# Inverting the 16x16 diagonal blocks of the delta matrices on VectorE, by way of DRAM, instead of four doubling levels on TensorE

## The chip, the cores and the metric

One core of one Trainium2 chip runs the whole program in one launch. The metric is device time in microseconds (us). TensorE multiplies matrices into PSUM, VectorE and ScalarE do elementwise work and empty PSUM, GpSimd does a little elementwise work and issues some DMAs, SyncE issues the weight loads. Engines run on their own and meet at semaphores.

## The reference, cut to what matters

A decoder block over T = 528 positions (16 meta tokens and 512 inputs), width 2048. Most of the work is projection: `proj = xn @ w_in` (2048 x 14368), two output projections and `w_o`. One branch is a gated delta rule with 16 heads of width 128, in NCH = 9 chunks of C = 64 positions. For each head and chunk a unit lower triangular 64x64 matrix is inverted:

```python
k_beta = k * beta[..., None]
lmat = jnp.where(strict, jnp.einsum('bhncd,bhnsd->bhncs', k_beta, k) * decay, 0.0)
tmat = lax.linalg.triangular_solve(eye + lmat, jnp.broadcast_to(eye, lmat.shape), left_side=True, lower=True)
u_c = jnp.einsum('bhncs,bhnsd->bhncd', tmat, v_beta)
w_c = jnp.einsum('bhncs,bhnsd->bhncd', tmat, k_beta * jnp.exp(gcum)[..., None])
```

Then a scan over the 9 chunks carries a 128x128 state per head.

## The kernel before, in words

**The main stream.** The projection runs in windows: for a column block `cp` of 256 weights, four windows (`c`, `h`), each of eight k tiles. A k tile takes three products (`wh*xh`, `wh*xl`, `wl*xh`, a weight and an input each split into a high and a low part), on two halves of 264 or 258 positions, or on one of 512. ScalarE makes `wh` (`split_hi`) and VectorE `wl` (`split_lo`) in four quarter pieces per window, for the window two ahead, in four buffers. SyncE loads 1 MB of raw weights for every second window, when VectorE has split the load before it in that buffer.

**Hooks.** After every second k tile `window` calls `hook(q)`, so a window has four hooks. The heads go in pairs: the four column blocks of a pair (k, q, v, z) have 64 hooks, and hook number m of pair p calls `delta(p - 1, m)` on TensorE, VectorE and ScalarE, which does one piece of the delta rule of the pair before. The last pair's pieces go into the first gate windows. Each engine's instructions stand in this written order; within a window the split comes first and then the hook, and the convolution (`convolve`, hooks 0 to 3 and 8 to 11 of a column block) last. So a wait in a hook holds back all that its engine has behind it. GpSimd's part runs in a loop of its own over the pairs.

**The inversion.** The two heads of a pair lie on partitions 0 to 63 and 64 to 127. `mq` holds decay times K K^T (and Q K^T) for the 9 chunks, `st` the inverse transposed with its column factor, `tm` the inverse. Hook F0 + 4 = 10 makes level 0 (pairs of rows) on VectorE from factors that GpSimd and a small product of hook 8 (`qd_shift`) prepare. From hook L0 = 13 on come levels of doubling, three hooks each: stage 2 of a level transposes `st` on TensorE and ScalarE copies it to `tm`; stage 0 of the next is `mq * tm`, masked by VectorE into `xm`; stage 1 is `xm * st`, subtracted by VectorE from `st`. Levels 1 to 3 take nine chunks, level 4 and 5 eight, level 5 in 32x32 quarters. At R0 = 28 the scan over the chunks begins, up to O0 = 55, and hook 61 is the last. The v and q transposes (`TOK_ROUNDS`) stand at hooks 13, 16, 19, 22, 25 and 28.

Of the kernel before, what the change touches and what calls it, by code (L numbers as in the profile page):

```python
# [52 lines left out]
LEVELS = 6  # L53
SHORT = 4
# [21 lines left out]
CPAIR = 258  # L76
CEPS = 322
# [3 lines left out]
NCOLS = CLEV + C * LEVELS  # L81
# [9 lines left out]
def constants():  # L91
# [10 lines left out]
    c[:, CPAIR:CPAIR + C] = (s[:, None] % 2 == 0) & (col[None] == s[:, None] + 1)  # L102
    for h in range(2):
        c[:, CHALF + h] = half == h
    for lv in range(LEVELS):
        a, b = s[:, None] >> lv, col[None] >> lv
        c[:, CLEV + C * lv:CLEV + C * (lv + 1)] = (b % 2 == 0) & (a == b + 1)
# [16 lines left out]
def build(nc, x, meta_tokens, norm_w, w_in, conv_w, A_log, dt_bias, pool_mix, pool_scale, dn_norm_w,  # L124
# [3 lines left out]
    g_d = nc.dram_tensor("gate_sum_scratch", (PAIRS, 2, NCH, C), F32, kind="Internal").ap()  # L128

    outer = ExitStack()  # L130
    with outer:
# [68 lines left out]
        pw, px = (vtok[:, :, i * C:(i + 1) * C] for i in range(2))  # L200
# [11 lines left out]
        lvm = lay.tensor("lvm", [LEVELS, C])  # L212
# [118 lines left out]
        pe_gate = sem("pe_gate")  # L331
# [161 lines left out]
        def _(pe):  # L493
# [104 lines left out]
            def delta(d, m):  # L598
# [23 lines left out]
                if m in TOK_ROUNDS:  # L622
# [3 lines left out]
                    if TOK_ROUNDS[m][0] == ("v", 0):  # L626
                        wait(silu_done, 4, 3)
                        wait(qd_pair, 1, 1)
# [4 lines left out]
                if m == F0 + 2:  # L633

                    wait(qd_ready, 1, 1)
                    wait(tok_done, ALL_TOK, K_TOK)
                    pe.wait_ge(masks_loaded, 16)
                    alone()
                    for ph in HALVES:
                        mm = product(pt[ph, 0:NCH], lvm[ph, 0, :], qd[ph, 1, :], True, True)  # L640
                    mm.then_inc(qd_shift, 1)
                lv, stage = level_step(m)
                if lv is not None:
                    for g in range(NG):
                        chunks = group(g, lv)
                        if stage == 0:

                            wait(t_ready, NG * (LEVELS - 1), NG * (lv - 1) + g + 1)
                            alone()
                        if stage == 1:  # L650
                            wait(x_ready, NG * (LEVELS - 1), NG * (lv - 1) + g + 1)
                            alone()
                        if stage == 2:
                            wait(s_ready, NG * LEVELS, NG * lv + g + 1)
                            if lv == 0 and g == 0:
                                wait(mq_ready, NG, NG)
                            alone()
                        for n in range(chunks.start, chunks.stop):
                            i = n - GC * g
                            if stage == 2:  # L660
                                mm = pe.transpose(pg[g][0:C, P * i:P * (i + 1)], st[:, n, :], ident)  # L661
                                continue
                            if lv == LEVELS - 1:
# [13 lines left out]
                        mm.then_inc((x_mm, y_mm, t_tr)[stage], 1)  # L677
# [143 lines left out]
        def _(act):  # L821
# [90 lines left out]
            def delta(d, m):  # L912
# [34 lines left out]
                lv, stage = level_step(m)  # L947
                if stage == 2:

                    for g in range(NG):  # L950
                        chunks = group(g, lv)
# [197 lines left out]
        def _(dve):  # L1149
# [170 lines left out]
            def delta(d, m):  # L1320
# [20 lines left out]
                if m == F0 + 1:  # L1341
# [7 lines left out]
                    wait(qd_ready, 1, 1)  # L1349
                    tt(st[:, :, :], cst[:, CI2:CI2 + C].unsqueeze(1).broadcast_to([P, NCH, C]), bc(qd[:, 1, :], C), ALU.mult).then_inc(s_init, 1)  # L1350

                if m == F0 + 2:
                    wait(qd_shift, 1, 1)
                    tt(qd[:, 2, :], pt[:, 0:NCH], qd[:, 1, :], ALU.mult).then_inc(qd_pair, 1)
                if m == F0 + 4:

# [351 lines left out]
```

## Time and profile before

| | us |
|---|---|
| median of 3 runs (lowest, highest) | 2143.07 (2142.34 to 2145.54) |
| span of the profiled execution | 2142.4 |
| TensorE matmul busy | 2096.9 (98%) |
| VectorE busy | 943.1 (44%) |
| ScalarE busy | 847.2 (40%) |
| GpSimd busy | 116.6 (5%) |
| GpSimd's DMA queue, share of 16 DMA engines | 2.7% |
| SyncE's DMA queue, share of 16 DMA engines | 25.8% |

The profiled execution is 0.7 us from the median. A pair of heads takes 135.5 us (from the first burst after hook 5 of one pair to that of the next, 892.64 to 1028.10). Times with two numbers are start and length in us; a matmul in fp32 leaves two records, so "x36" are 18 products.

### The profile page before, as it was taken

What the parts mean: (1) busy time and instruction counts of PE and PEld (TensorE: products, weight loads), DVE (VectorE), ACT (ScalarE), POOL (GpSimd) and SP (SyncE); (2) the same over time, 40 slices, a digit from 0 to 9 for tenths busy, and PEclk for the clock granted to TensorE, in tenths of its full rate; (3) what the DMA queues carried; (4) which work ended last, traced back from release to release, by engine and by line L of the source; (5) the groups of instructions that cost most, each with busy time, mean ns of one, the idle gap of its engine ahead of it and who ended that gap; (6) DMA issues with size and microseconds to landing.
All of it is one profiled execution on the core that took longest, in us unless ns stands there. A gap on an engine that the chain in (4) does not pass through costs nothing.

```text
span 2142.4 us, 40278 instructions
## 1 busy us (share of the span) xinstructions
PE 2096.9 (98%) x15140; PEld 1805.1 (84%) x15140; DVE 943.1 (44%) x2391; ACT 847.2 (40%) x2476; POOL 116.6 (5%) x139
## 2 busy tenths in 40 slices
PE   6999999999999999999999999999999999999996
PEld 6888899989889798897988987778888888888885
DVE  6333444545555455554555544332222544334333
ACT  5322224445354453543535436432222522223333
POOL 4000000000010000100001000000000000000000
PEclk9999999999999999999999999999999999999998
DMA  6133322122121221212212122243346343435221
GB/s 219 54 125 102 98 80 80 61 76 80 41 95 60 76 76 44 95 59 72 66 60 95 41 84 84 76 131 120 103 140 227 113 128 117 147 126 217 79 78 78
DMA packets 177340, 209.06 MB, mean 98 GB/s; under 512 B 6793, under 2 KB 163298, under 8 KB 176546
## 3 DMA queue, kind: packets, MB, share of 16 engines
q1 hardware_dynamic: 167090, 180.27, 25.8%
q0 software_dynamic: 5504, 18.33, 2.7%
q10 hardware_dynamic: 4608, 8.39, 1.0%
q8 instruction: 115, 1.88, 0.4%
q14 instruction: 23, 0.19, 0.0%
HBM read 188.05 MB, written 18.91 MB: 97 GB/s over the span
## 4 chain that ended last, share of the span: by engine, by line
PE 96%; ACT 1%; issue 1%; DVE 1%; POOL 0%; SPq 0%; DMA 0%; DVEq 0%; ACTq 0%
PE pj L495 81%; PE pg L495 9%; PE pt L495 2%; PE pg L661 2%; PE pt L631 1%; ACT tm L823 0%; PE pg L782 0%; DVE fst L1180 0%; POOL xl L1619 0%; ACT pt L946 0%; DMA prow<-in_dn_norm_w 0%; PE pt L725 0%; PE pg L725 0%; DVE res L1599 0%; DVE xl L1186 0%
## 5 line engine op out<-in xcount | busy, mean ns | idle before, releaser
L495 PE MATMUL pj<-xh,wh 128*128 128x264 f32 (+2 forms) x2688 | 756.6, 336 | 4.1 <-DVE wl L1155 3.0
L495 PE MATMUL pj<-xh,wl 128*128 128x264 f32 (+2 forms) x2688 | 716.9, 321 | 6.0 <-issue 6.0
L495 PE MATMUL pj<-xl,wh 128*128 128x264 f32 (+2 forms) x2688 | 718.9, 322 | 0.0
L1155 DVE TENSOR_TENSOR wl<-raw,wh 128x256 fp32r<-128x256 f32 x896 | 365.5, 439 | 678.4 <-ACT wh L823 678.3
L495 PEld LDWEIGHTS pj<-xh,wh 128*128 128x128 f32 x2688 | 445.4, 189 | 71.0 <-issue 26.4
L495 PEld LDWEIGHTS pj<-xh,wl 128*128 128x128 f32 x2688 | 447.5, 189 | 44.9 <-issue 6.6
L495 PEld LDWEIGHTS pj<-xl,wh 128*128 128x128 f32 x2688 | 447.2, 189 | 34.7 <-issue 1.0
L823 ACT ACTIVATE wh<-raw 128x256 fp32r<-128x256 f32 x896 | 310.6, 406 | 20.4 <-ACT stg L1000 19.3
L823 ACT ACTIVATE wh<-rawb 128x256 fp32r<-128x256 f32 x288 | 97.8, 406 | 182.2 <-PE pj L495 181.2
L495 PE MATMUL pj<-yh,wh 128*128 128x512 f32 x384 | 149.6, 389 | 0.0
L495 PE MATMUL pj<-yh,wl 128*128 128x512 f32 x384 | 149.5, 389 | 0.0
L495 PE MATMUL pj<-yl,wh 128*128 128x512 f32 x384 | 149.5, 389 | 0.0
L1318 DVE SCALAR_TENSOR_TENSOR stg<-xin,convcur,stg 128x528 f32<-128x528 f32 x144 | 112.4, 780 | 0.2
L1470 DVE TENSOR_TENSOR wl<-rawb,wh 128x256 fp32r<-128x256 f32 x192 | 69.6, 420 | 92.2 <-ACT wh L823 92.2
L495 PE MATMUL pj<-mh,wh 128*128 128x512 f32 x256 | 101.3, 396 | 0.0
L961 ACT ACTIVATE oo<-pt,cur 128x128 f32<-128x128 f32 x64 | 23.5, 368 | 195.5 <-PE pt L495 195.5
L495 PE MATMUL pj<-mh,wl 128*128 128x512 f32 x256 | 99.9, 390 | 0.0
L495 PE MATMUL pj<-ml,wh 128*128 128x512 f32 x256 | 99.9, 390 | 0.0
L1000 ACT ACTIVATE stg<-pj 128x512 f32<-128x512 f32 x32 | 19.1, 597 | 174.4 <-PE pj L495 174.4
L495 PEld LDWEIGHTS pj<-yh,wl 128*128 128x128 f32 x384 | 72.1, 188 | 15.1
L495 PEld LDWEIGHTS pj<-yh,wh 128*128 128x128 f32 x384 | 72.1, 188 | 15.0
L495 PEld LDWEIGHTS pj<-yl,wh 128*128 128x128 f32 x384 | 72.1, 188 | 14.8
(202 smaller groups left out, 1904.0 us busy)
## 6 DMA issues: line engine op xcount, KB each, us to landing
raw<-in_w_in SPq DMA_DIRECT2D x112, 1024.0 KB, 5.2
rawb<-in_w_dn_out SPq DMA_DIRECT2D x16, 1024.0 KB, 5.8
rawb<-in_w_o SPq DMA_DIRECT2D x12, 1024.0 KB, 5.5
gates_scratch<-stg ACTq DMA_DIRECT2D x32, 256.0 KB, 2.0
rawb<-in_w_pool_out SPq DMA_DIRECT2D x8, 1024.0 KB, 5.6
gst<-gates_scratch POOLq DMA_DIRECT2D x32, 256.0 KB, 3.0
yraw<-branch_scratch SPq DMA_DIRECT2D x1, 5632.0 KB, 21.4
xt<-in_x SPq DMA_DIRECT2D x4, 1024.0 KB, 7.0
```

What stands on the lines that cost most here:

```text
L495: return pe.matmul(dst, lhs, rhs, start=start, stop=stop)
L631: mm = pe.transpose(pt[:, i * P:(i + 1) * P], src.rearrange("p h c -> p (h c)"), ident)
L661: mm = pe.transpose(pg[g][0:C, P * i:P * (i + 1)], st[:, n, :], ident)
L823: return act.activation(dst, src, ACT.Copy)
L961: act.activation(oo[:, n - 1, :], pt[:, 0:HD], ACT.Copy, scale=cur[:, EG, n:n + 1]).then_inc(o_inter, 1)
L1000: act.activation(gates_sb[c], pj[c][:, 0, :], ACT.Sigmoid).then_inc(proj_evac, 1)
L1155: tt(wl[:, j, 2 * q:2 * q + 2, :], raw[:, 2 * par + h, 2 * q:2 * q + 2, c * P:(c + 1) * P], wh[:, j, 2 * q:2 * q + 2, :].bitcast(F32), ALU ...
L1318: dve.scalar_tensor_tensor(acc, xin[:, src_tap:src_tap + T], w, acc, ALU.mult, ALU.add).then_inc(conv_step, 1)
L1470: tt(bwl[:, u, 2 * q:2 * q + 2, :], rawb[:, u, 2 * q:2 * q + 2, c * P:(c + 1) * P], bwh[:, u, 2 * q:2 * q + 2, :].bitcast(F32), ALU.subtra ...
```

## The change

The inverse of each 64x64 matrix now starts from the inverses of its four 16x16 diagonal blocks; levels 4 and 5 remain. A pair has 2 heads x 9 chunks x 4 blocks = 72 blocks. VectorE scales K K^T by the factor `qd` (one instruction, hook 10), GpSimd stores it to a scratch tensor in DRAM in rows of 256 bytes and loads the blocks back, one block of 256 numbers in each of 72 partitions, in runs of 64 bytes. From hook W0 = 13 on VectorE inverts them by columns: 14 steps of two dependent instructions, three steps per hook, and then a turned copy. GpSimd stores the inverse and its transpose (runs of 64 bytes) into two scratch tensors, whose other places were zeroed once at the start, and loads them as `tm` and `st` (rows of 256 bytes). TensorE waits for all four loads at hook L0 = 24. Level 4 gets small products that update `tm`, in place of the transposes. R0, O0, the token rounds and the main stream stay. The column factor moves into ScalarE's copy to `vn`. The blocks lie in `oo`, which the scan writes only later.

```diff
--- before.py
+++ after.py
...
-LEVELS = 6
-SHORT = 4
+LEVELS = (4, 5)
+NL = len(LEVELS)
+BS = 16
+NB = C // BS
+NBLK = NCH * 2 * NB
+BROW = BS * C + BS
...
+    gram_d = nc.dram_tensor("gram_scratch", (NBLK, BROW), F32, kind="Internal").ap()
+    inv_d = [nc.dram_tensor(f"inverse_scratch{i}", (NBLK, BROW), F32, kind="Internal").ap() for i in range(2)]
...
-        pw, px = (vtok[:, :, i * C:(i + 1) * C] for i in range(2))
+        flat = oo[0:NBLK, :, :].rearrange("p n e -> p (n e)")
+        gblk, wblk, wtr = (flat[:, i * BS * BS:(i + 1) * BS * BS].rearrange("p (a i) -> p a i", a=BS) for i in range(3))
+        tblk = flat[:, 3 * BS * BS:4 * BS * BS]
...
-        L0 = F0 + 7
+        V0 = F0 + 7
+        W0 = F0 + 7
+        NSTEP = 3
+        L0 = W0 + 11
...
-            TOK_ROUNDS[L0 + 3 * i] = [("v", n) for n in range(3 * i, 3 * i + 3)]
-            TOK_ROUNDS[L0 + 9 + 3 * i] = [("q", n) for n in range(3 * i + 1, min(3 * i + 4, NCH))]
+            TOK_ROUNDS[V0 + 3 * i] = [("v", n) for n in range(3 * i, 3 * i + 3)]
+            TOK_ROUNDS[V0 + 9 + 3 * i] = [("q", n) for n in range(3 * i + 1, min(3 * i + 4, NCH))]
...
-            return ((m - L0 + 2) // 3, (m - L0 + 2) % 3) if L0 <= m < R0 else (None, None)
-
-        R0 = L0 + 3 * LEVELS - 3
+            return ((m - L0) // 2, (m - L0) % 2) if L0 <= m < R0 else (None, None)
+
+        R0 = L0 + 2 * NL
...
-                if m == F0 + 2:
-
-                    wait(qd_ready, 1, 1)
-                    wait(tok_done, ALL_TOK, K_TOK)
-                    pe.wait_ge(masks_loaded, 16)
-                    alone()
-                    for ph in HALVES:
-                        mm = product(pt[ph, 0:NCH], lvm[ph, 0, :], qd[ph, 1, :], True, True)
-                    mm.then_inc(qd_shift, 1)
...
+                    if (lv, stage) == (0, 0):
+                        wait(inv_loaded, 64, 64)
+                        pe.wait_ge(masks_loaded, 16)
+                        alone()
...
-                        if stage == 2:
-                            wait(s_ready, NG * LEVELS, NG * lv + g + 1)
-                            if lv == 0 and g == 0:
-                                wait(mq_ready, NG, NG)
...
-                            if stage == 2:
-                                mm = pe.transpose(pg[g][0:C, P * i:P * (i + 1)], st[:, n, :], ident)
-                                continue
...
-                        mm.then_inc((x_mm, y_mm, t_tr)[stage], 1)
+                        mm.then_inc((x_mm, y_mm)[stage], 1)
+                        if (lv, stage) == (0, 1):
+                            for n in range(chunks.start, chunks.stop):
+                                i = n - GC * g
+                                for low, high in QUARTERS:
+                                    mm = product(pg[g][low, 384 + 32 * i:416 + 32 * i], st[low, n, 0:32], xm[low, n, 0:32], True, True)
+                            mm.then_inc(t_mm, 1)
...
-                    for g in range(NG):
-                        chunks = group(g, lv)
-                        wait(t_tr, NG * (LEVELS - 1), NG * lv + g + 1)
-                        for hd in range(2):
-                            src = pg[g][0:C, 0:GC * P].rearrange("p (n h c) -> p n h c", h=2, c=C)[:, chunks.start - GC * g:, hd, :]
-                            ins = copy(tm[HALVES[hd], chunks, :], src)
-                        ins.then_inc(t_ready, 1)
...
-                        copy(vn[:, :], pg[0][:, 128:128 + HD]).then_inc(vn_ready, 1)
+                        act.activation(vn[:, :], pg[0][:, 128:128 + HD], ACT.Copy, scale=qd[:, 1, n:n + 1]).then_inc(vn_ready, 1)
...
-                    tt(st[:, :, :], cst[:, CI2:CI2 + C].unsqueeze(1).broadcast_to([P, NCH, C]), bc(qd[:, 1, :], C), ALU.mult).then_inc(s_init, 1)
...
-                        tt(px[:, group(g), :], kk, pw[:, group(g), :], ALU.mult).then_inc(pair_x, 1)
-                    for g in range(NG):
-                        wait(pair_x, NG, g + 1)
-                        tt(st[:, group(g), :], st[:, group(g), :], px[:, group(g), :], ALU.subtract).then_inc(s_ready, 1)
...
+                if m == F0 + 4:
+                    wait(qd_ready, 1, 1)
+                    wait(mq_ready, NG, NG)
+                    tt(mq[:, :, 0, :], mq[:, :, 0, :], bc(qd[:, 1, :], C), ALU.mult).then_inc(mk_ready, 1)
+                if m == W0:
+
+                    wait(blk_loaded, 16, 16)
+                    dve.tensor_scalar(wblk, gblk, -1.0, None, ALU.mult).then_inc(w_init, 1)
+                    wait(w_init, 2, 1)
+                    dve.memset(wblk.rearrange("p a i -> p (a i)")[:, 0:BS * BS:BS + 1], 1.0).then_inc(w_init, 1)
+                    wait(w_init, 2, 2)
+                if W0 <= m and 1 + NSTEP * (m - W0) < BS - 1:
+                    for j in range(1 + NSTEP * (m - W0), min(1 + NSTEP * (m - W0 + 1), BS - 1)):
+                        rest = BS - 1 - j
+                        own = tblk[:, 0:j * rest].rearrange("p (a i) -> p a i", a=j)
+                        if j > 1:
+                            wait(w_step, BS - 2, j - 1)
+                        tt(own, wblk[:, 0:j, j:j + 1].broadcast_to([NBLK, j, rest]),
+                           gblk[:, j:j + 1, j + 1:BS].broadcast_to([NBLK, j, rest]), ALU.mult).then_inc(w_prod, 1)
+                        wait(w_prod, BS - 2, j)
+                        tt(wblk[:, 0:j, j + 1:BS], wblk[:, 0:j, j + 1:BS], own, ALU.subtract).then_inc(w_step, 1)
+                    if j == BS - 2:
+                        wait(w_step, BS - 2, BS - 2)
+                        dve.tensor_copy(wtr, wblk.rearrange("p a i -> p i a")).then_inc(w_turned, 1)
...
+                        elif lv == 0:
+
+                            wait(t_mm, NG, g + 1)
+                            tt(st[:, chunks, :], st[:, chunks, :], src, ALU.subtract).then_inc(s_ready, 1)
+                            for low, high in QUARTERS:
+                                part = tm[low, chunks, 0:32]
+                                move = pg[g][low, 384:480].rearrange("p (n c) -> p n c", c=32)[:, chunks.start - GC * g:, :]
+                                ins = tt(part, part, move, ALU.subtract)
+                            ins.then_inc(t_ready, 1)
...
-                pool.wait_ge(decay_exp, d + 1)
-                pool.tensor_tensor(pw, dec[:, :, :], cst[:, CPAIR:CPAIR + C].unsqueeze(1).broadcast_to([P, NCH, C]), ALU.mult).then_inc(pair_dec, 1)
-                pool.wait_ge(pair_dec, d + 1)
-                pool.wait_ge(qd_pair, d + 1)
-                pool.tensor_tensor(pw, pw, bc(qd[:, 2, :], C), ALU.mult).then_inc(pair_fac, 1)
+                def rows_of(scratch, h):
+
+                    return scratch.rearrange("(n h b) r -> n h (b r)", h=2, b=NB)[:, h, 0:C * C].rearrange("n (s c) -> s n c", c=C)
+
+                pool.wait_ge(mk_ready, d + 1)
+                pool.sem_inc(pool_gate, 1)
+                for h in range(2):
+                    pool.dma_start(rows_of(gram_d, h), mq[HALVES[h], :, 0, :]).then_inc(mk_stored, 16)
+                pool.wait_ge(mk_stored, 32 * d + 32)
+                pool.sem_inc(pool_gate, 1)
+                pool.dma_start(gblk, gram_d[:, 0:BS * C].rearrange("a (j c) -> a j c", c=C)[:, :, 0:BS]).then_inc(blk_loaded, 16)
+
+                pool.wait_ge(w_turned, d + 1)
+                pool.sem_inc(pool_gate, 1)
+                for scratch, block_of in zip(inv_d, (wblk, wtr)):
+                    pool.dma_start(scratch[:, 0:BS * C].rearrange("a (j c) -> a j c", c=C)[:, :, 0:BS], block_of).then_inc(w_stored, 16)
+                pool.wait_ge(w_stored, 32 * d + 32)
+                pool.sem_inc(pool_gate, 1)
+                for h in range(2):
+                    pool.dma_start(tm[HALVES[h], :, :], rows_of(inv_d[1], h)).then_inc(inv_loaded, 16)
+                    pool.dma_start(st[HALVES[h], :, :], rows_of(inv_d[0], h)).then_inc(inv_loaded, 16)
```

On TensorE, hooks 13 and 14 of a pair before (`pt<-cst,vch` are the v transposes, `pg<-cst,st` the transposes of `st`, `pg<-tm,mq` stage 0 of level 1):

```order
L121 REGISTER_ALU
L631 MATMUL pt<-cst,vch 128x128 x3
L121 ISA x2
L661 MATMUL pg<-cst,st 64x128 x3
L121 REGISTER_ALU
L661 MATMUL pg<-cst,st 64x128 x3
L121 REGISTER_ALU
L661 MATMUL pg<-cst,st 64x128 x3
L495 MATMUL pj<-xh,wh 128x264 x2
```

The same engine in the changed kernel, the end of hook 23 and hook 24, where the wait for the four loads stands ahead of the first product of level 4:

```order
L508 MATMUL pj<-xh,wh 128x258 x2
L508 MATMUL pj<-xl,wh 128x258 x2
L508 MATMUL pj<-xh,wl 128x258 x2
L125 ISA
L508 MATMUL pg<-tm,mq 64x64 x16
L508 MATMUL pj<-xh,wh 128x258 x2
```

Hooks 13 to 23 now hold the v and q transposes alone, and the levels' products begin at hook 24.

On GpSimd, from the decay difference (`dec`) to the first scaled copy of `st` (`sq`), before:

```order
L1656 TENSOR_TENSOR dec<-tm,cur 128x576
L1659 TENSOR_TENSOR vtok<-dec,cst 128x9x64
L1662 TENSOR_TENSOR vtok<-vtok,qd 128x9x64
L1664 ISA
L1665 TENSOR_TENSOR sq<-st,cst 128x384
```

and in the changed kernel:

```order
L1670 TENSOR_TENSOR dec<-tm,cur 128x576
L1679 DMA gram_scratch<-mq 64x9x64 x2
L1682 DMA oo<-gram_scratch 72x16x16
L1687 DMA inverse_scratch<-oo 72x16x16 x2
L1691 DMA tm<-inverse_scratch 64x9x64
L1692 DMA st<-inverse_scratch 64x9x64
L1691 DMA tm<-inverse_scratch 64x9x64
L1692 DMA st<-inverse_scratch 64x9x64
L1694 ISA
L1695 TENSOR_TENSOR sq<-st,cst 128x384
```

Nine DMAs in four groups, each group behind a wait, stand where two elementwise instructions stood.

On VectorE in the changed kernel, the first hook of the inversion (m = 13) and the split of the next hook (`oo` holds the blocks):

```order
L125 ISA
L1357 TENSOR_SCALAR oo<-oo 72x256
L1359 MEMSET oo 72x16
L1367 TENSOR_TENSOR oo<-oo 72x14
L125 ISA
L1370 TENSOR_TENSOR oo<-oo 72x14
L1367 TENSOR_TENSOR oo<-oo 72x26
L125 REGISTER_ALU
L1370 TENSOR_TENSOR oo<-oo 72x2x13
L1367 TENSOR_TENSOR oo<-oo 72x36
L125 REGISTER_ALU
L1370 TENSOR_TENSOR oo<-oo 72x3x12
L1149 REGISTER_ALU
L1150 TENSOR_TENSOR wl<-raw,wh 128x256
```

The wait for the blocks (the first row) stands ahead of these and so ahead of every later split `wl`.

## Rows read from the trace of the kernel before

**Rows 1.** The page: busy time by engine, and the chain that ended last.

```profile
PE 2096.9 (98%) x15140; PEld 1805.1 (84%) x15140; DVE 943.1 (44%) x2391; ACT 847.2 (40%) x2476; POOL 116.6 (5%) x139
PE 96%; ACT 1%; issue 1%; DVE 1%; POOL 0%; SPq 0%; DMA 0%; DVEq 0%; ACTq 0%
```

**Rows 2.** Waits, longest in total: us, times, longest us.

```profile
DVE wl L1155 <- ACT wh L823: 678.3, 261, 9.8
```

**Rows 3.** Chain of waits, hooks 13 to 27 of one pair: start, us.

```profile
904.75 0.33 PE pt L631 x3
905.08 0.98 PE pg L661 x9
906.06 1.45 PE pj L495 x12
907.51 1.20 PE pg L495 x36
908.70 1.67 PE pj L495 x12
910.37 1.20 PE pg L495 x36
...
935.60 1.08 PE pg L495 x32
...
943.73 0.62 PE pg L495 x32
```

**Rows 4.** Timeline of VectorE, hooks 7 to 10 of the same pair.

```profile
895.89 0.17 DVE L1346 TENSOR_TENSOR qd<-cur,rk 128x9 f32<-128x9 f32 x1
896.10 0.17 DVE L1348 TENSOR_TENSOR qd<-qd,rk 128x9 f32<-128x9 f32 x1
896.30 0.76 DVE L1350 TENSOR_TENSOR st<-cst,qd 128x576 f32<-128x576 f32 x1
897.57 0.50 DVE L1315 TENSOR_SCALAR stg<-xin,convcur 128x528 f32<-128x528 f32 x1
901.35 0.41 DVE L1155 TENSOR_TENSOR wl<-raw,wh 128x256 fp32r<-128x256 f32 x1
```

**Rows 5.** Groups by line: GpSimd's DMA issues, busy us and mean ns of one.

```profile
L1682 POOL DMA_DIRECT2D gst<-gates_scratch x32 | 17.2, 538 | 482.5 <-DMA gates_scratch<-stg 270.6 <-DVE merged L1495 211.2
L1647 POOL DMA_DIRECT2D tm<-gate_sum_scratch x16 | 8.4, 528 | 31.3 <-issue 30.8
L1606 POOL DMA_DIRECT2D mixcur<-in_pool_mix x4 | 3.1, 776 | 0.4 <-issue 0.4
L1630 POOL DMA_DIRECT2D gate_sum_scratch<-grow x2 | 1.3, 632 | 0.0
```

**Rows 6.** DMA issues: KB each, median us from issue to landing.

```profile
raw<-in_w_in SPq DMA_DIRECT2D x112, 1024.0 KB, 5.2
gst<-gates_scratch POOLq DMA_DIRECT2D x32, 256.0 KB, 3.0
tm<-gate_sum_scratch POOLq DMA_DIRECT2D x16, 144.0 KB, 2.9
gate_sum_scratch<-grow POOLq DMA_DIRECT2D x2, 18.0 KB, 4.0
```

**Rows 7.** The tile mixcur (256 KB by GpSimd, four loads): landing.

```profile
DMA to landing us min/median/max: 3.2/6.6/7.4
```

**Rows 8.** DMA queue of the weight loads: packets, MB, share of 16 engines.

```profile
q1 hardware_dynamic: 167090, 180.27, 25.8%
```

**Rows 9.** Stretches at the start: length, busy by engine, granted clock (PEclk), DMA.

```profile
27.00:30.00 3.00, 1.07 (x6) 1.11 (x7) 3.00 (x5) 1.19 (x2) 1.11 (x2) 0.83 1.09 386
33.00:36.00 3.00, 0.45 (x3) 0.45 (x4) 2.97 (x6) 2.67 (x6) 2.78 (x3) 0.97 0.01 3
36.00:39.00 3.00, 3.00 (x15) 3.00 (x15) 3.00 (x4) 3.00 (x11) 3.00 (x3) 0.50 0.02 5
39.00:42.00 3.00, 3.00 (x26) 3.00 (x25) 1.97 (x7) 0.46 (x2) 3.00 (x3) 0.96 0.00 0
```

More of the change, by code:

```diff
@@ L75 @@
 CHALF = 256
-CPAIR = 258
-CEPS = 322
+CEPS = 258
 NCONST = CEPS + 1
@@ L80 @@
 CLEV = CHB + P
-NCOLS = CLEV + C * LEVELS
+CZERO = CLEV + C * NL
+NZERO = NBLK * BROW // P
+NCOLS = CZERO + NZERO
 NTILE_CONV = 3 * HEADS
@@ L101, in constants @@
     c[:, CUP:CUP + C] = np.where(s[:, None] <= col[None], 0.0, NEG)
-    c[:, CPAIR:CPAIR + C] = (s[:, None] % 2 == 0) & (col[None] == s[:, None] + 1)
     for h in range(2):
         c[:, CHALF + h] = half == h
-    for lv in range(LEVELS):
+    for i, lv in enumerate(LEVELS):
         a, b = s[:, None] >> lv, col[None] >> lv
-        c[:, CLEV + C * lv:CLEV + C * (lv + 1)] = (b % 2 == 0) & (a == b + 1)
+        c[:, CLEV + C * i:CLEV + C * (i + 1)] = (b % 2 == 0) & (a == b + 1)
     same = half[:, None] == half[None]
@@ L1348, in delta @@
                     tt(qd[:, 1, :], qd[:, 0, :], rk[:, 1, :], ALU.mult).then_inc(qd_ready, 1)
-                    wait(qd_ready, 1, 1)
-                    tt(st[:, :, :], cst[:, CI2:CI2 + C].unsqueeze(1).broadcast_to([P, NCH, C]), bc(qd[:, 1, :], C), ALU.mult).then_inc(s_init, 1)
[L1352 to L1355, printed above, removed]
-                    wait(pair_fac, 1, 1)
-                    wait(s_init, 1, 1)
-                    for g in range(NG):
-                        kk = pg[g][:, 0:GC * 2 * C].rearrange("p (n a c) -> p n a c", a=2, c=C)[:, :, 0, :]
-                        tt(px[:, group(g), :], kk, pw[:, group(g), :], ALU.mult).then_inc(pair_x, 1)
-                    for g in range(NG):
-                        wait(pair_x, NG, g + 1)
-                        tt(st[:, group(g), :], st[:, group(g), :], px[:, group(g), :], ALU.subtract).then_inc(s_ready, 1)
                 if m == F0 + 3:
@@ L1377, in delta @@
                         if stage == 0:
-                            wait(x_mm, NG * (LEVELS - 1), NG * (lv - 1) + g + 1)
+                            wait(x_mm, NG * NL, NG * lv + g + 1)
+                            if (lv, g) == (0, 0):
+                                dve.wait_ge(masks_loaded, 16)
                             pattern = lvm[:, lv, :].unsqueeze(1).broadcast_to([P, chunks.stop - chunks.start, C])
                             tt(xm[:, chunks, :], src, pattern, ALU.mult).then_inc(x_ready, 1)
-                        else:
-                            wait(y_mm, NG * (LEVELS - 1), NG * (lv - 1) + g + 1)
-                            wait(s_ready, NG * LEVELS, NG * (lv - 1) + g + 1)
-                            if lv == LEVELS - 1:
-                                for low, high in QUARTERS:
-                                    part = st[low, chunks, 32:C]
-                                    ins = tt(part, part, src[low, :, 32:C], ALU.subtract)
-                                ins.then_inc(s_ready, 1)
-                            else:
-                                tt(st[:, chunks, :], st[:, chunks, :], src, ALU.subtract).then_inc(s_ready, 1)
+                        elif lv == 0:
[6 more added lines that the diff above has]
+                            ins.then_inc(t_ready, 1)
+                        else:
+                            wait(y_mm, NG * NL, NG * lv + g + 1)
+                            wait(s_ready, NG * NL, g + 1)
+                            for low, high in QUARTERS:
+                                part = st[low, chunks, 32:C]
+                                ins = tt(part, part, src[low, :, 32:C], ALU.subtract)
+                            ins.then_inc(s_ready, 1)
                 if R0 <= m < O0:
@@ L1639, in _ @@
             pool.memset(vch[:, 0, :, 0:PAD], 0.0).then_inc(zeroed, 1)
-            pool.dma_start(lvm[:, :, :], consts[:, CLEV:NCOLS].rearrange("p (l c) -> p l c", l=LEVELS)).then_inc(masks_loaded, 16)
+            pool.dma_start(lvm[:, :, :], consts[:, CLEV:CZERO].rearrange("p (l c) -> p l c", l=NL)).then_inc(masks_loaded, 16)
+            for i in range(2):
+                pool.dma_start(inv_d[i].rearrange("a r -> (a r)").rearrange("(p c) -> p c", p=P), consts[:, CZERO:NCOLS]).then_inc(blk_zeroed, 16)
             def row_load(d):
@@ L1649, in _ @@
             pool.wait_ge(gsum_stored, 32)
+            pool.wait_ge(blk_zeroed, 32)
             pool.sem_inc(work_free, 1)
```

36 lines of the change are left out of this document (17 added, 19 removed).

## The prediction

> **What bounds the kernel now.** I read the page first: TensorE is busy 98% of the span, and the chain that ended last runs 96% through it [rows 1]. The waits say that nobody else presses: VectorE's longest sum of waits, 678 us, is for ScalarE's high parts, and ScalarE makes those only as TensorE frees buffers [rows 2]. So every product that leaves TensorE's queue shortens the span, and every us that TensorE waits lengthens it. Then I read one pair of heads in the chain of waits [rows 3]: bursts of small products stand between the stretches `pj` of the projection, and ScalarE's and VectorE's part of a level fits under the next stretch. TensorE has no reserve of other work at a wait: its queue is in order.
>
> **What the change takes from TensorE, per pair.** From rows 3:
> - transposes of `st` at hooks 13, 16, 19, 22: 4 x 0.98; at hook 25 eight of them, 8/9 of that, 0.87. Together 4.8 us.
> - stages 0 and 1 of levels 1 to 3: six bursts "x36" of 1.20 = 7.2 us. The stretch behind such a burst lasts 1.67, that behind the transposes 1.45, so each burst costs another 0.2: 1.2 us.
> - the small product of hook 8, about 0.2, and a short wait for ScalarE's copies at level 5, about 0.2.
>
> Sum 13.6 us. Added: sixteen 32x32 products at hook 25; a burst of level 5 is as many of that size, 0.62. Net 13.0 us per pair, 8 pairs: 104 us. This is the most that the change can bring: 2143 - 104 = 2039.
>
> **What it puts in its place.** TensorE must have all four loads before hook 24. Follow one pair on the clock of rows 3 and 4.
>
> TensorE's deadline. Hook 24's burst began at 935.6. Ahead of it go 3.9 of transposes, 8.4 of bursts, 0.2 of hook 8 and the burst of hook 23 (1.16 and 0.2, now in hook 24): 13.8. So TensorE would stand at hook 24 at 921.8. Each us that the loads land later is a wait s, and a pair changes by s - 13.0.
>
> The start. VectorE began the split of hook 10 at 901.35 [rows 4]. The instruction of 576 elements at hook 7 (0.76) and a small one go; behind the split (0.41) comes the scaling of K K^T, again 576 elements, 0.76. It ends at 901.35 - 0.9 + 0.41 + 0.76 = 901.6.
>
> From there a chain without a fork: stores A, load B, the inversion C, stores D, loads E. No DMA of before has 576 or 1152 runs, so A, B, D and E are bounded. Issue time on GpSimd: 528 ns for 64 runs, 538 for 128, 632 for 72, 776 for 256 (`mixcur`, two per partition) [rows 5]. Per further run that is 0.16 ns (64 to 128), 0.78 (72 to 256) or 1.86 (128 to 256). I take the middle of the two larger, since these copies too have several runs in a partition: 1.2 us for 576 runs (1.0 to 1.4), 1.95 for 1152 (1.5 to 2.4). From the end of an issue to landing: 3.0 - 0.54 = 2.5 for loads (`gst`), 4.0 - 0.63 = 3.4 for the store of small rows into DRAM (`grow`, 256 bytes) [rows 5, 6].
> - A, two stores of 576: 2.4 + 3.4 = 5.8.
> - B, one load of 1152: 1.95 + 2.5 = 4.4.
> - C, VectorE: a dependent instruction follows the last after 0.21 us (895.89, 896.10, 896.30), and 0.76 against 0.17 for 567 elements more makes 1.04 ns per element [rows 4]. 28 instructions, 1120 elements together: 28 x 0.21 + 0.9 = 6.8. Negation of 256 elements 0.4 (a `wl` of 256 is 0.41), diagonal 0.2, turned copy 0.4. Between them in the same queue four splits of 0.41 and one tap of the convolution, 0.50: 2.2. Sum 10.0.
> - D, two stores of 1152: 3.9 + 3.4 = 7.3.
> - E, four loads of 576: 4.8 + 2.5 = 7.3.
> - Weight loads of 1 MB (5.2 us each, rows 6) share the DMA engines. `mixcur` landed after 3.2 at best and 7.4 at worst [rows 7]. VectorE's splits of hooks 19 and 23 release a load each, and they fall behind the inversion, so beside D and E. I count one such delay: 4.2.
>
> Chain 39.0 us: the loads land at 940.6, s = 18.8, and the pair is 18.8 - 13.0 = 5.8 us longer.
>
> VectorE's own hold. It stands at hook 13 from about 906 until B lands near 912, with the splits of hooks 14 to 19 behind it; those of hooks 12 to 15 feed TensorE's window of hooks 20 to 23, which starts near 914, those of hooks 16 to 19 the next, from hook 24. TensorE so waits a little twice, but ahead of the deadline: these waits are part of s. ScalarE waits for none of it, and the copies that it loses were hidden. GpSimd has nothing else until `sq`.
>
> The clock. At the start, where TensorE was idle for most of 27 to 36 us, it got 0.83 and 0.97, and then, busy the whole of 36 to 39, 0.50, which is 1.2 GHz; from 39 to 42 it had 0.96 again [rows 9]. After a wait of more than ten us I expect the same, 3 us at half speed for 1.5, and a bit on the level's products: 2.0 us (0 to 3).
>
> Sum: 5.8 + 2.0 = 7.8 per pair, 8 pairs, 62 us on the profiled 2142.4, and 0.7 more for the median: **2205 us**. The two zeroing stores run before the first pair, where GpSimd is idle, and cost nothing.
>
> **What the Trainium skill says.** The Trainium skill, "DMA: Bandwidth & Descriptors", section on the anatomy of one DMA, says that a DMA on GpSimd's path takes about 2.0 us and its bytes at 436 GB/s, with the making of descriptors small. By it A, B, D and E would be 2.7, 2.2, 2.3 and 3.4, the chain 20.6, s 0.4, and the time, as an estimate, about 2042. The trace has 2.9 for 144 KB, where the rule has 2.3 [rows 6]. The same page's table of specifications says that below 512 bytes the DMA engines read, modify and write; no row here shows a write of 64 bytes.
>
> **Rivals.**
> - *Only the number of round trips counts* (faster). The rows for it are those of 64 and 128 runs, whose issue differs by 10 ns, and 2.9 us for 144 KB. With 0.53 per issue and 2.4 to landing, A 3.5, B 2.9, D 3.5, E 4.5, C 9.0 and no weight load in the way: chain 23.4, landing at 925.0, s = 3.2, 9.8 us saved per pair: 2143 - 78 = 2065. Against it stands that 256 runs cost 0.24 more than 128. It decides where the chain is under some 31 us. Chance 0.27. (The Trainium skill's page of the paragraph above has the same case, at 2042.)
> - *The DMA engines pay for each run* (slower still). The weight queue's 167,090 packets took 25.8% of 16 engines over 2142 us, 53 ns for a packet of 1 KB [rows 8]. If a run of 64 or 256 bytes costs the same, 72 runs per engine last 3.8 us, and 144 last 7.6. A grows by 1.4, B by 1.9, D by 3.7, E by 2.8: chain 48.8, s = 28.6, a pair + 17.6 with the clock, 2284. Weight loads in all four groups would give 12.6 more, up to 2385. Chance 0.24.
> - *The forecast*, chains of 34 to 45 us: 0.45. A chain within half a us of 31.2, where the wait and its 2.0 of clock eat up the 13.0, leaves the time within 0.2% (about 4 us, what a measurement of this kernel can tell from no change): 0.04.
>
> **How the numbers follow.** Time is 2143 + 8 x (chain - 33.2 + clock): one us of chain is 8 us of the result, so small costs per run move it far, and both signs are possible. The likeliest case's own range is 2150 to 2255. The range for 8 in 10 reaches from the round trip case, 2062, to past the per run case, 2325. Slower 0.69 (forecast's 0.45 and the second rival's 0.24), same 0.04, faster 0.27.
>
> **What would show it.** In the changed kernel's trace: hooks 13 to 23 as nearly bare stretches of 1.45 us with TensorE at hook 24 some 14 us sooner (right if so); one TensorE wait per pair at the first product of level 4, put down to the DMA of `tm` or `st`, of 14 to 24 us (a wait under 11 means faster); issues of GpSimd near 1.2 and 1.95 us; VectorE's chain near 10 us; VectorE's wait at the negation near 6 us; granted clock under 1.00 in each pair behind the wait. The prediction is wrong if issues or landings of many short runs cost no more than those of few, or if they cost several times as much.

## The result, and the profile after

The changed kernel takes 2152.93 us (2151.83 to 2154.69, 4 runs), the kernel before, beside it, 2143.58 (2142.34 to 2145.54, 4 runs): 1.0045 of the time, 95% interval 1.0031 to 1.0059. It is slower by 9.4 us. The forecast was slower by 62.

The page of the changed kernel: busy time by engine, then the chain that ended last, by engine.

```profile
PE 2015.4 (94%) x13284; PEld 1731.0 (80%) x13284; DVE 934.4 (43%) x2487; ACT 778.4 (36%) x2236; POOL 158.0 (7%) x197
...
PE 85%; DMA 6%; DVE 4%; issue 3%; POOL 1%; ACT 1%; SPq 0%; DVEq 0%; ACTq 0%; POOLq 0%
```

TensorE has 81.5 us less work than in [rows 1] and yet the span is 10.7 longer (2153.1): it now waits. The waits say where (us in total, times, longest).

```profile
PE pg L508 <- DMA st<-inverse_scratch: 93.1, 8, 12.7
```

That is 11.6 us per pair. The chain of waits through one pair, start and us (compare [rows 3], where no engine but TensorE stands in this place); "issue" is time for which the trace shows no wait:

```profile
768.31 0.77 DVE mq L1353
769.11 0.57 issue
769.69 0.79 POOL gram_scratch L1679
770.47 2.74 DMA gram_scratch<-mq
773.25 0.71 issue
773.96 3.43 DMA oo<-gram_scratch
777.41 0.30 DVE oo L1357
...
785.73 0.40 DVE oo L1373
786.17 0.60 issue
786.77 1.02 POOL inverse_scratch L1687
787.80 8.77 DMA inverse_scratch<-oo
796.61 0.53 issue
797.14 0.76 POOL tm L1691
...
799.37 3.09 DMA st<-inverse_scratch
802.60 1.97 PE pg L508 x32
```

The reader sees the five steps of the sum: A from 769.1 (the end of VectorE's scaling) to 773.96, B to 777.41, C to 786.77, D to 797.14, E to 802.60. That they belong to one path, from K K^T to the first product of level 4, is what the chain shows: 33.5 us, each step released by the one before. Between an engine's wait and its next DMA stand 0.5 to 0.7 us that no transfer fills (the rows "issue"). The longest of the five is D, 10.4 us. Over the eight pairs it is 9.2: 2.0 of issue, and the 7.2 that GpSimd waits behind it (57.3 in all).

GpSimd's issues by group (busy us, mean ns of one, idle before), which answer to [rows 5]:

```profile
L1687 POOL DMA_DIRECT2D inverse_scratch<-oo x16 | 16.2, 1019 | 94.0 <-DVE oo L1373 94.0
L1679 POOL DMA_DIRECT2D gram_scratch<-mq x16 | 12.3, 772 | 109.4 <-DVE mq L1353 109.4
L1691 POOL DMA_DIRECT2D tm<-inverse_scratch x16 | 12.0, 748 | 57.3 <-DMA inverse_scratch<-oo 57.3
L1692 POOL DMA_DIRECT2D st<-inverse_scratch x16 | 11.9, 742 | 0.0
...
L1682 POOL DMA_DIRECT2D oo<-gram_scratch x8 | 8.5, 1067 | 22.2 <-DMA gram_scratch<-mq 19.1 <-issue 3.0
```

576 runs take 742 to 772 ns to issue, 1152 runs 1019 to 1067. Against the 528 of 64 runs [rows 5] that is 0.42 to 0.50 ns per further run. It is no law for all shapes: `mixcur` took 776 ns for 256 runs [rows 5], as long as 576 runs here.

Issue to landing (KB each, median us), which answers to [rows 6]:

```profile
gram_scratch<-mq POOLq DMA_DIRECT2D x16, 144.0 KB, 2.7
...
inverse_scratch<-oo POOLq DMA_DIRECT2D x16, 72.0 KB, 6.6
...
oo<-gram_scratch POOLq DMA_DIRECT2D x8, 72.0 KB, 3.5
```

And D's stretch in the DMA view, 786.7 to 797.2: two weight loads are under way beside the block stores, and their queue (q1) takes 61% of the engines.

```profile
q1 hardware_dynamic: 2011, 2.03, 61.1%
q0 software_dynamic: 96, 0.15, 12.1%
```

The clock in that pair (stretch, length, busy of PE, PEld, DVE, ACT, POOL, granted clock, DMA share, GB/s), which answers to [rows 9]:

```profile
790.00:794.00 4.00, 0.00 (x0) 0.00 (x0) 0.50 (x2) 0.07 (x1) 0.00 (x0) 1.00 0.91 277
794.00:798.00 4.00, 0.00 (x0) 0.00 (x0) 0.00 (x0) 0.00 (x0) 0.85 (x2) 0.57 0.74 256
798.00:802.00 4.00, 0.00 (x0) 0.00 (x0) 0.00 (x0) 0.00 (x0) 2.11 (x3) 0.50 0.56 153
802.00:806.00 4.00, 3.40 (x39) 3.31 (x40) 1.74 (x5) 0.00 (x0) 0.00 (x0) 0.50 0.01 4
806.00:810.00 4.00, 4.00 (x62) 3.40 (x61) 0.99 (x5) 1.86 (x10) 0.00 (x0) 0.72 0.00 0
```

TensorE idles from 790 on, falls to 1.2 GHz, and still works its first 5.6 us behind the wait at that level (3.4 busy in the row at 0.50, and 0.28 x 4 / 0.5 = 2.2 in the next).

What a pair takes is read from GpSimd's store of `sz`, which comes once per pair. The first and the seventh, six pairs apart, of the kernel before and then of the changed one:

```profile
472.39 0.77 POOL L1669 DMA_DIRECT2D branch_scratch<-sz  x1 [65.03 <-DVE sz L1439]
...
1283.61 0.77 POOL L1669 DMA_DIRECT2D branch_scratch<-sz  x1 [65.01 <-DVE sz L1439]
```

```profile
474.17 0.80 POOL L1699 DMA_DIRECT2D branch_scratch<-sz  x1 [65.00 <-DVE sz L1450]
...
1292.50 0.80 POOL L1699 DMA_DIRECT2D branch_scratch<-sz  x1 [65.00 <-DVE sz L1450]
```

135.2 us per pair before, 136.4 after: 1.2 more.

### The profile page after: what moved, and what is told of

It is laid out like the page before. It is cut to its first block, busy times and chain, and to the rows that moved or that the text cites. A ratio compares the mean times of both kernels' runs of the same rounds, so it can differ in the third digit from the quotient of the medians.

```text
span 2153.1 us, 35910 instructions
## 1 busy us (share of the span) xinstructions
PE 2015.4 (94%) x13284; PEld 1731.0 (80%) x13284; DVE 934.4 (43%) x2487; ACT 778.4 (36%) x2236; POOL 158.0 (7%) x197
## 4 chain that ended last, share of the span: by engine, by line
PE 85%; DMA 6%; DVE 4%; issue 3%; POOL 1%; ACT 1%; SPq 0%; DVEq 0%; ACTq 0%; POOLq 0%
PE pj L508 74%; PE pg L508 7%; DMA inverse_scratch<-oo 3%; PE pt L508 2%; DMA st<-inverse_scratch 1%; DVE oo L1367 1%; PE pt L643 1%; DVE oo L1370 1%; DMA oo<-gram_scratch 1%; DMA gram_scratch<-mq 1%; DVE wl L1150 0%; POOL tm L1691 0%; POOL inverse_scratch L1687 0%; DVE mq L1348 0%; PE pg L787 0%
## 5 line engine op out<-in xcount | busy, mean ns | idle before, releaser
L1150 DVE TENSOR_TENSOR wl<-raw,wh 128x256 fp32r<-128x256 f32 x896 | 354.6, 429 | 542.5 <-ACT wh L828 542.3
L508 PE MATMUL pg<-tm,mq 32*32 32x32 f32 (+1 forms) x512 | 21.3, 253 | 93.1 <-DMA st<-inverse_scratch 93.1
L508 PEld LDWEIGHTS pg<-tm,mq 32*32 32x32 f32 (+1 forms) x512 | 19.2, 164 | 96.1 <-issue 95.2
L951 ACT ACTIVATE pt<-pt 128x128 f32<-128x128 f32 x64 | 17.0, 266 | 194.4 <-PE pt L643 194.4
```

The costliest lines, as they stand in the source:

```text
L508: return pe.matmul(dst, lhs, rhs, start=start, stop=stop)
L951: act.activation(src, src, ACT.Square, accum_out=norms[:, 1, n:n + 1]).then_inc(tok_done, 1)
L1150: tt(wl[:, j, 2 * q:2 * q + 2, :], raw[:, 2 * par + h, 2 * q:2 * q + 2, c * P:(c + 1) * P], wh[:, j, 2 * q:2 * q + 2, :].bitcast(F32), ALU ...
```

## The experiments

Each row is a kernel beside the one before on the same chip; "vs after" is against 2152.9. The kernel before had medians of 2140.9 to 2143.6 in these comparisons, so 1 to 2 us in the column "vs after" say nothing. Where there is no interval, it is one run.

| kernel | median us | ratio to before (95%) | vs after | TensorE's wait for the inverse, per pair |
|---|---|---|---|---|
| loads that depend on nothing | 2041.5 | 0.9526 (0.951 to 0.9542) | -111 | none |
| weight loads held | 2125.7 | 0.9916 (0.99 to 0.9933) | -27 | 8.4 |
| filler for the clock | 2139.8 | 0.9993 (0.9977 to 1.0008) | -13 | 2.0 |
| block stores once more, in a quiet place | 2156.2 | | +3 | 11.7 |
| level 4 one hook later | 2135.4 | 0.9963 (0.995 to 0.9977) | -18 | 9.8 |
| held, and D in runs of 1 KB | 2101.6 | | -51 | 5.5 |
| all steps in one hook | 2148.4 | 1.002 (1.0009 to 1.0031) | -5 | 6.3 |
| four edits together (8) | 2077.7 | 0.97 (0.9686 to 0.9713) | -75 | none |
| the four, but three steps per hook | 2098.1 | 0.9796 (0.9779 to 0.9812) | -55 | 5.3 |
| the four, but seven steps per hook | 2076.3 | 0.9697 (0.968 to 0.9713) | -77 | 0.1 |

**1. Loads that depend on nothing.** The four loads read two other scratches that hold zeros, right behind the load of the blocks; the inversion and its stores still run, but nothing waits for them, and levels 4 and 5 work on zeros instead of the blocks' inverses.

```diff
+                for h in range(2):
+                    pool.dma_start(tm[HALVES[h], :, :], rows_of(idle_d[1], h)).then_inc(inv_loaded, 16)
+                    pool.dma_start(st[HALVES[h], :, :], rows_of(idle_d[0], h)).then_inc(inv_loaded, 16)
                 pool.wait_ge(w_turned, d + 1)
...
-                for h in range(2):
-                    pool.dma_start(tm[HALVES[h], :, :], rows_of(inv_d[1], h)).then_inc(inv_loaded, 16)
-                    pool.dma_start(st[HALVES[h], :, :], rows_of(inv_d[0], h)).then_inc(inv_loaded, 16)
```

> The four loads read two other DRAM tensors, zeroed once, and are issued right behind the load of the blocks, so that TensorE no longer depends on the inversion; all else, the inversion and its stores too, stays (the diagonal inverses don't reach levels 4 and 5 in it). Theory: the change takes 13.0 us per pair from TensorE, and gives 11.6 (the mean wait for the loads in the trace) and some 2.3 of clock back. Then this kernel has no wait for a DMA at hook 24, a granted clock of 1.00, and 2040 us (2143.6 - 104; 2034 to 2046). Rival: the removed products were worth less, or VectorE's hold at hook 13 starves TensorE of low parts: 2060 us or more, with TensorE waits for wl at hooks 20 and 24.

2041.5 us, granted clock 0.994 as before. The same two stores of `sz`:

```profile
459.63 0.81 POOL L1701 DMA_DIRECT2D branch_scratch<-sz  x1 [65.00 <-DVE sz L1451]
...
1193.28 0.81 POOL L1701 DMA_DIRECT2D branch_scratch<-sz  x1 [65.01 <-DVE sz L1451]
```

122.3 us per pair, 12.9 less than before (the sum had 13.0), and 14.1 less than with the real chain: 11.6 of it is the wait, and 2.5 is left. I put it on the clock behind the wait; experiment 5 tests that.

**2. Weight loads held.** SyncE waits for the four loads before it starts the weight loads of the fourth column block (and of the second gate iteration), which in the changed kernel run beside D.

```diff
-            with sp.Fori(0, PAIRS) as p:
+            def load_pair(p, hold):
...
+                    if k == 3 and hold:
+                        sp.wait_ge(inv_loaded, 64 * p)
```

> SyncE holds the weight loads that fell beside the stores of the inverses until the four loads of that pair have landed; nothing else changes. Theory one: the stores land 7.2 us after their issue because two weight loads of 1 MB share the DMA engines with them, where the stores of K K^T needed 2.7. Then they land after 2.7 to 3.5, the wait shrinks by about 4 us per pair, and the time is 2117 us (2110 to 2125). Theory two: 2304 runs of 64 bytes written to DRAM take that long by themselves: landing stays at 6 to 8, time 2149 to 2157.

2125.7, just above the range that was expected (2110 to 2125). The block stores landed sooner and so did the wait behind them end (first the view of DMA issues, then GpSimd's group of the first load, with its idle time before):

```profile
inverse_scratch<-oo POOLq DMA_DIRECT2D x16, 72.0 KB, 4.2
```

```profile
L1704 POOL DMA_DIRECT2D tm<-inverse_scratch x16 | 12.0, 749 | 31.5 <-DMA inverse_scratch<-oo 31.5
```

57.3 fell to 31.5, 3.2 us per pair: that is what the weight loads cost D. 3.9 is left, where the stores of K K^T, twice the bytes, need 2.8 (22.2 in 8). The stores' queue in D's stretch of one pair here (776.9 to 783.2):

```profile
q0 software_dynamic: 96, 0.15, 28.7%
```

28.7% of 16 engines over 6.3 us is 1.8 us per engine, for 144 runs of 64 bytes: 13 ns a run, in packets of 24 runs (2304 runs in 96 packets).

**3. The same, and D in runs of 1 KB.** Each block goes as one run of 256 numbers instead of 16 runs of 16. The matrices loaded are then not the inverses; the amount of work is unchanged.

```diff
-                    pool.dma_start(scratch[:, 0:BS * C].rearrange("a (j c) -> a j c", c=C)[:, :, 0:BS], block_of).then_inc(w_stored, 16)
+                    pool.dma_start(scratch[:, 0:BS * BS].rearrange("a (j c) -> a j c", c=BS), block_of).then_inc(w_stored, 16)
```

> As e3_weights_held, but each block of the inverse goes to DRAM as one run of 1 KB in place of 16 runs of 64 bytes (the loads read the same places as before, so the inverses that they bring are wrong). If the short runs are what is left of the slow landing, it falls from 3.9 us after the issue to the 2.7 of the stores of K K^T, and the issue from 1.02 us to about 0.6 each. If runs cost nothing, both stay.

GpSimd's groups, and then the DMA issue:

```profile
L1704 POOL DMA_DIRECT2D tm<-inverse_scratch x16 | 12.1, 755 | 16.3 <-DMA inverse_scratch<-oo 16.3
...
L1700 POOL DMA_DIRECT2D inverse_scratch<-oo x16 | 8.7, 549 | 93.4 <-DVE oo L1386 93.4
```

```profile
inverse_scratch<-oo POOLq DMA_DIRECT2D x16, 72.0 KB, 2.0
```

Same bytes, 1/16 of the runs: an issue falls from 1019 to 549 ns, a landing from 4.2 to 2.0 us, the wait behind D from 31.5 to 16.3. That makes 2 x 0.47 + 1.9 = 2.8 us per pair for the short runs in D, and the pair became 2.9 shorter (129.7 against 132.5, both from `sz`). The wait behind D fell to 2.0 us, where 2.7 was expected: a miss in size. The Trainium skill, "DMA: Bandwidth & Descriptors", table of specifications, says that below 512 bytes the DMA engines read, modify and write; the landing halves here with 1 KB runs (4.2 to 2.0 us), which agrees in direction, but these runs can't tell that from a price per run.

**4. The block stores once more, in a quiet place.** Two further stores of the same shape, before the inversion starts, to a scratch of their own.

```diff
+                pool.wait_ge(blk_loaded, 16 * d + 16)
+                pool.sem_inc(pool_gate, 1)
+                for scratch in dup_d:
+                    pool.dma_start(scratch[:, 0:BS * C].rearrange("a (j c) -> a j c", c=C)[:, :, 0:BS], gblk).then_inc(dup_stored, 16)
```

> While VectorE inverts and no weights are loaded, GpSimd stores the raw blocks to two further DRAM tensors with the same 64 byte runs as the real stores. Weights theory: these copies land 3 to 4 us after the start of their issue, the real ones still 6 to 7 (6.6 median in the changed kernel). Run theory: the copies take 6 to 9 us too. Time about 2153 either way, since GpSimd is idle there.

The tile of the extra stores, from issue to landing, and the real ones in the same run:

```profile
DMA to landing us min/median/max: 3.5/4.3/5.2
```

```profile
inverse_scratch<-oo POOLq DMA_DIRECT2D x16, 72.0 KB, 6.4
```

4.3 against 6.4 for a transfer of the same shape, and 4.2 with the weights held: the neighbours explain the difference, and some 4.3 is the transfer's own.

**5. Filler for the clock.** 80 products whose results nobody reads stand ahead of the wait.

```diff
+                        wait(mq_ready, NG, NG)
+                        for _ in range(80):
+                            product(pg[0][:, 0:HALF], xh[:, 0, 0:P], xh[:, 0, 0:HALF], True, True)
```

> Ahead of its wait at hook 24 TensorE makes 80 products of 264 columns into a free PSUM bank (9.7 us, the mean wait is 11.6), whose results nobody reads. Theory: 2.3 us per pair of the change's cost are TensorE's clock after the wait. With the filler the granted clock stays at 1.00 around hook 24, and the time is 2135 us (2130 to 2141). Rival: the clock is not what costs them: 2153 us, or more by the filler's overhang.

13 us came back (11 by the two ratios to before), 1.4 to 1.6 per pair, of the 2.5. The filler covers the wait up to its last 2.8 us in the pair shown (stretches of 4 us as above), and in this pair clock is still lost behind it. In the pair before, a wait of 2.7 us up to 663.0 lost none (third row):

```profile
794.00:798.00 4.00, 1.20 (x22) 1.01 (x22) 0.00 (x0) 0.00 (x0) 0.99 (x2) 1.00 0.42 123
798.00:802.00 4.00, 4.00 (x39) 3.75 (x34) 1.74 (x5) 0.00 (x0) 0.00 (x0) 0.58 0.00 0
...
663.00:667.00 4.00, 3.96 (x72) 3.65 (x73) 1.91 (x6) 0.80 (x6) 0.00 (x0) 1.00 0.00 0
```

So part of the price is the clock, 1.4 to 1.6 of it; the rest of the 2.5 did not come back. It fits that four of the eight pairs still ran at the lower level behind the wait that was left.

**6. Level 4 one hook later.** `L0 = W0 + 12`, so one more stretch of projection stands ahead of the wait.

> Levels 4 and 5 and all behind them stand one hook later (L0 from 24 to 25). If the time is set by how long TensorE waits at that hook, a hook of 1.45 us more of projection ahead of it takes that much off the wait: 8 x 1.45 = 11.6 us, 2141 us (2137 to 2145). Rival: what costs is not the wait itself but the scan behind it, which now also ends a hook later: no gain, 2151 or more.

17.5 us saved, 2.2 per pair, more than expected. The wait fell by 1.85 (78.3 in all) and the mean clock rose from 0.968 to 0.973. The expectation had counted the hook's 1.45 us of projection alone. Hook 25 also holds q transposes, and in the trace they now stand ahead of the wait: 0.33 us [rows 3], 1.78 together. The other 0.3 fits the clock, but was not tested. A shift by two hooks was not run, since the last piece of a pair would fall past its last hook.

**7. All steps of the inversion in one hook.** `NSTEP = 14`: no splits and taps between the steps.

> All 14 steps of the inversion stand in hook 13 (NSTEP 14), so that four splits and a tap of the convolution no longer lie between them. Theory: only the chain up to hook 24 counts; it is 1.8 us shorter per pair, 14 us in all: 2139 us (2134 to 2144). Rival: the splits of hooks 14 and 15 come 5 us later and starve TensorE at hook 20, and that is not hidden: 2153 or more.

Only some 5 us, against 14 expected, and still slower than before. The wait for the inverse fell by 5.3 per pair, but little of that is gain. TensorE's waits, and the place in one pair:

```profile
PE pg L508 <- DMA st<-inverse_scratch: 50.6, 8, 8.0
PE pj L508 <- DVE wl L1150: 30.8, 9, 4.7
```

```profile
783.64 0.51 PE L508 MATMUL pj<-xh,wh 128*128 128x258 f32 x2 [3.29 <-DVE wl L1150]
```

In the changed kernel the waits for `wl` are 4.1 in all; here they are 30.8, 3.3 more per pair, since VectorE makes no split from 775.6 to 782.8. So TensorE only comes to hook 24 later. And the clock falls a second time per pair, to 0.60 behind this wait of 3.3 us:

```profile
784.00:788.00 4.00, 4.00 (x24) 4.00 (x23) 4.00 (x10) 0.00 (x0) 1.93 (x2) 0.60 0.41 33
```

E, which was clear of the weight loads, now meets them:

```profile
tm<-inverse_scratch POOLq DMA_DIRECT2D x16, 144.0 KB, 5.2
st<-inverse_scratch POOLq DMA_DIRECT2D x16, 144.0 KB, 6.1
```

They had 3.0 and 3.2. The collision moved from D (4.5 here) to E. Over the eight pairs C fell from 9.3 to 8.0 us and D from 9.2 to 7.7, but E grew from 5.5 to 8.2 (read from the starts in both traces): the chain stayed at 32.3, where it had 32.4. That is why the 1.8 us that the expectation took off the chain did not become time. D's own issues grew too, from 1019 to 1157 ns each, while VectorE works off its late splits; the cause of that is open.

**8. Four edits together.** Weight loads held, level 4 at hook 25, `NSTEP = 14`, and both loads of `tm` issued ahead of those of `st`, with a semaphore of their own; stage 1 alone waits for `st`.

```diff
-        NSTEP = 3
-        L0 = W0 + 11
+        NSTEP = 14
+        L0 = W0 + 12
...
-                        wait(inv_loaded, 64, 64)
+                        wait(tm_loaded, 32, 32)
...
+                            if (lv, g) == (0, 0):
+                                wait(inv_loaded, 32, 32)
```

> Four steps together: weight loads held until the loads of the inverses have landed, levels 4 and 5 one hook later, all 14 steps in hook 13, and the two loads of tm issued first, with TensorE's wait for st only at the second product of level 4. From the mean wait of e3_weights_held, 8.4 us, go 1.45 (a hook), 1.8 (splits) and 1.5 (two issues): 3.7 us per pair are left, and little of the clock. 2041.5 + 8 x 3.7 + 0 to 16: 2079 us (2068 to 2092). Rival: TensorE now waits for low parts at hook 20 instead, since VectorE is held there: 2100 or more.

2077.7, as expected, and 3% faster than the kernel before. TensorE no longer waits for the inverse; what is left is the wait for the splits (30.9 in all) at hook 20, which the rival had named, without the time that the rival gave it.

**9. Three or seven steps per hook in that kernel.** Is the wait for the splits now the cost, or does the chain to `tm` set the pair?

> As the kernel of all four edits, but three steps of the inversion per hook again. There TensorE waited 3.2 us for VectorE's splits at hook 20 and ran the 4 us behind it at a granted clock of 0.61; the loads of tm landed at 768.0 and the first product of level 4 ran at 768.2. With three steps per hook the splits are in time again (no such wait), but the block stores start 1.4 us later (four splits and a tap between the steps), so tm lands at about 769.4 and TensorE waits there instead: for 769.4 - 763.5 = 5.9 us, with the slow clock on the products behind it. A pair ends about 1.2 us later for tm and about 0.5 more for the slow products: theory that the chain from K K^T to tm alone sets the pair: 2078 + 8 x 1.4 = 2089 (2082 to 2096), with a TensorE wait of 5 to 6 us per pair on the DMA of tm. Rival, that the wait for the splits was the cost and the loads had slack: 2078 - 8 x 3 = 2054.

> As the kernel of all four edits, but seven steps per hook, so in two hooks, with the split of hook 14 between them. If the chain to tm alone sets the pair: stores start about 0.5 us later than with all steps in one hook, the wait at hook 20 shrinks or goes, and the time is 2078 + 8 x 0.5 = 2082 (2075 to 2088). Rival, that the splits' wait was the cost: under 2065.

With three steps the splits are in time and the wait for `tm` is back:

```profile
PE pg L522 <- DMA tm<-inverse_scratch: 42.6, 8, 7.1
```

2098.1 rules out that the splits' wait was the cost (that would have given 2054), but it lies above the 2082 to 2096 of the chain alone. From B's issue to D's it is 12.8 us here and 11.5 with fourteen steps, and the wait of 5.3 is near the 5.9 expected. Of that 1.3 little arrives: from the end of the scaling to the first product of level 4 a pair takes 27.8 us here and 27.5 with fourteen steps (mean of seven pairs, from the starts in both traces). The clock is the larger part, by where it falls. Stretches of one pair, first with fourteen steps (the splits' wait ends at 757.4, the level's first product is at 768.2), then with three (first product at 776.0):

```profile
756.00:760.00 4.00, 2.58 (x12) 2.58 (x13) 3.93 (x11) 0.02 (x1) 2.34 (x2) 0.61 0.20 16
...
768.00:772.00 4.00, 4.00 (x75) 3.48 (x73) 2.35 (x7) 1.85 (x9) 0.00 (x0) 1.00 0.38 92
```

```profile
776.00:780.00 4.00, 4.00 (x44) 3.88 (x44) 2.02 (x5) 0.00 (x0) 0.00 (x0) 0.58 0.37 97
```

With fourteen steps TensorE is slow while the chain is still on its way, so that the loss is hidden; with three it is slow behind the first product, 0.42 x 4 = 1.7 us of full speed in this pair, 2.2 in the mean of the eight. 0.3 and 2.2 make the 2.5 per pair, 20 us, that the two kernels are apart. With seven, 2076.3, no different from fourteen (the intervals overlap) and inside what was expected; but its splits are waited for as long (30.4 in all), where a shorter wait was expected. It and the kernel of experiment 8 are the best versions of this study.

## Why the prediction was wrong in size

Direction and mechanism held, the size did not: 2205 forecast, 2152.9 measured, so the margin over before was 9 us and not 62. Step by step:

- **TensorE's saving, 13.0 per pair:** right, 12.9 measured with the wait taken out (experiment 1).
- **The place and kind of the price:** right. One wait per pair at the first product of level 4, put down to the load of `st`; 11.6 us where 14 to 24 was given.
- **The failed step is the issue time on GpSimd,** in the words "I take the middle of the two larger": 1.2 us for 576 runs and 1.95 for 1152, from 0.78 and 1.86 ns per further run. Measured are 0.74 to 0.77 and 1.02 to 1.07 us, 0.42 to 0.50 ns per further run. Nine issues in the chain were to take 2.4 + 1.95 + 3.9 + 4.8 = 13.05 us and took 1.54 + 1.06 + 2.03 + 2.98 = 7.6. A pair was to become 7.8 longer and became 1.2 longer; 5.4 of these 6.6 us are the issues, 0.7 is C and 0.4 is D behind its issue. The rows of before bounded the slope from 0.16 to 1.86, and the value lay between the two smaller ones; `mixcur`'s 776 ns for 256 runs, which pulled the choice up, is no guide to these shapes; why it costs as much as 576 runs here stays open.
- **From the end of an issue to the next step, in A, B and E:** 3.4, 2.4 and 2.5 us in the pair shown, where the sum had 3.4, 2.5 and 2.5. **C:** 9.4 against 10.0 (9.3 in the mean).
- **D and the weight loads:** "I count one such delay: 4.2" was right in kind and near in sum: 7.2 us behind D's issue, against 3.4 + 4.2 = 7.6. The parts differ: the weights cost 3.2 (experiment 2), the 64-byte runs 1.9 of the rest (experiment 3). The pair shown is a bad one, 8.3.
- **VectorE's own hold, "TensorE so waits a little twice":** did not occur, though VectorE waited 6.0 us at the negation, as forecast. TensorE's waits for `wl` are 4.1 us in the whole changed kernel. Experiment 7 shows when it does: with the steps unbroken.
- **The clock, 2.0 per pair:** 2.5 left over in experiment 1, of which the filler returned 1.4 to 1.6.
- **The rivals:** that only round trips count gave 2065; it failed, since the issues and landings of short runs do cost more, 2.8 us per pair in D alone. That each run costs the DMA engines 53 ns gave 2284; it failed too: with the weights held D's stores were done 3.9 us behind their issue, not 3.4 + 3.7, and took the engines 13 ns a run (experiment 2). The 53 ns were for a packet of 1 KB, and a packet holds 24 of the short runs. The mean chain is 32.4, past the point of 31.2 where the sign turns and short of the 34 to 45 of the forecast: a gap for which the three cases had no name.

## What to carry to other kernels

When a change trades work of the busiest engine for a chain of dependent transfers, the result is chain minus slack, times the number of rounds: first find the point where the sign turns, and spend the care on the term that is multiplied most often, here the cost of an issue per run. A chain that ends a few us late is worth mending before it is given up: delaying two weight loads, moving the deadline by one hook and loading first what is needed first turned 1.0045 into 0.98, and merged steps on top of them made it 0.97. Merging steps alone gave 1.002: it pays only where the work pushed behind them, and the transfers which it releases, have room.

## What the runs showed of the hardware

- A DMA issue on GpSimd took 549 ns for 72 runs of 1 KB, 772 for 576 of 256 bytes, 1019 for 1152 of 64 bytes: twice the runs with half the bytes cost more. But 256 runs took 776 in `mixcur` [rows 5], so the number of runs alone does not give it.
- 72 KB stored to DRAM landed in 2.0 us in 1 KB runs, 4.2 in 64-byte runs, and 6.6 in 64-byte runs beside two weight loads of 1 MB.
- Stores of 64-byte runs took the DMA engines 13 ns a run (28.7% of 16 engines over 6.3 us for 2304 runs), 24 runs to a packet.
- A clock loss ahead of a deadline that a chain sets was hidden (1.8 us per pair, experiment 8); the loss behind it, 2.2 us per pair, showed in the time (experiment 9).
- A TensorE wait of 2.8 us was followed by 4 us at a granted clock of 0.58 (experiment 5), one of 12.7 by 0.50 and then 0.72. Summed over those rows the short one lost 0.42 x 4 = 1.7 us of full speed, the long one 0.50 x 3.4 + 0.28 x 4 = 2.8. In the same trace a wait of 2.7 us was followed by 1.00, so the length of the wait alone does not decide.
